# Reordered first loads, conditioning sums and weight splits in a fused mixer block

## The chip, the cores and the metric

The kernel runs on one core of a Trainium2 chip. The time is the device time of one execution in microseconds; three executions of the kernel before gave 1876.54, 1878.39 and 1878.52 us, with a median of 1878.39 us. Everything is float32 in and out.

## The reference: what is computed

One layer over a sequence of 4096 rows of 1024 numbers. A conditioning vector c makes a shift, a scale and a gate for each of the 1024 columns, each a product of silu(c) with a third of w_ada (1024 x 3072). The rows are normalised, scaled and shifted, and go through one wide projection; two branches (causal pooling, and a chunkwise recurrent memory with four heads) read its columns; their outputs are joined, projected by w_out, gated, added to x and normalised again.

```python
mod = jax.nn.silu(c) @ w_ada[l] + b_ada[l]
shift, scale, gate = jnp.split(mod, 3, axis=-1)
h = rms_norm(x, norm_g[l]) * (1.0 + scale[:, None, :]) + shift[:, None, :]
proj = h @ w_in[l]
...
x = x + gate[:, None, :] * (mix @ w_out[l])
```

## The kernel before, in words

The sequence is cut into 8 blocks of 512 rows. For each block the normalised, modulated rows are turned so that columns lie on partitions (`hT`), multiplied with `w_in` tile by tile, run through the branches and multiplied with `w_out`. Large products are made of three passes: a value is split into a rounded high part and a low part (the rest), and high x high, high x low and low x high are added. So each weight tile and each piece of `hT` has a high part, made by ScalarE (`split_w`, `hi_first`), and a low part, made by GpSimd (`low_w`, `lo_first`), in this order.

Each engine has its own instruction stream, written out by hand, and streams meet at semaphores. Nothing reorders them: an engine that waits holds everything behind it. The change touches only what is done once, before and during the first product of the first block. There the streams are these.

SyncE issues nearly all loads, and its queue moves them in the order of issue: the constants `cst`; seven small parameter vectors into rows of `hm` (`norm_g`, `c`, `b_ada`, `conv_w`, `conv_b`, `ls_pool`, `mh_norm_g`, L391); x's row chunks 0 and 1 (L371); groups 0 and 1 of w_ada (`load_ada`, L396, 1 MB each); x's chunks 2 and 3; group 2; the raw V weights 0 and 1 (`load_raw`, L336 for the small gate columns and L344); group 3; V weights 2 and 3; and then groups 4 to 7 and V weights 4 to 7 in turns. Chunks 2 and 3 wait until ScalarE has squared a first and a second chunk.

Groups 0 to 3 of w_ada make the shift and scale of columns 0 to 511, groups 4 to 7 those of columns 512 to 1023. A group has 8 row tiles of 128. VectorE folds tiles 0 to 4 into one by scaling with silu(c) (`sum_ada`: one multiplication, L1239, and four multiply-adds, L1242), and TensorE multiplies tiles 5, 6 and 7 with silu(c) (L540) and adds the folded tile through a product with ones (L543). It does so for two column halves of a group, one after the other, and waits for VectorE's sum before the first L543. The constant `ADA_SUMMED = 5` is the number of folded tiles.

VectorE's stream, in order: variance of chunks 0 and 1 (`prep_var`, L1187), sums of groups 0 and 1, variance of chunks 2 and 3, sums 2 and 3, `modulation(0)` (L1253 to L1257), `full_first(0)` and `(1)`, sum 4, `full_first(2)`, sum 5, `full_first(3)`, sums 6 and 7, `modulation(1)`, `full_first(4)` to `(7)`, then the sums of the gate. `full_first(i)` (L1270) applies scale and shift to one turned chunk half.

ScalarE: the tanh of silu(c) (L836), which needs the parameters; squares of chunks 0 and 1 (L826), their scaling (L841); squares of chunks 2 and 3, their scaling; splits of V weights 0 to 3; then the high parts of the chunk halves (L846), with one further V weight split (L822) before each of the halves 2 to 5. GpSimd follows with the low parts (L1083, L1108) in the same order.

TensorE: transposes of chunks 0 and 1, `ada(0)` (groups 0, 1), `ada(1)` (2, 3), three transposes, V weights 0 to 3 on chunks 0 and 1, `ada(2)` (4, 5), V weights 0 to 3 on chunks 2 and 3 with `ada(3)` (6, 7) after the second, and so on to the end of V; then the tiles of q.

Of the kernel before, what the change touches and what calls it, by code (L numbers as in the profile page):

```python
# [34 lines left out]
P = 128  # L35
D = 1024
KT = D // P
# [17 lines left out]
V_HELD = 4  # L55
UNITS = V_UNITS + 2 * 24
TILE_UNITS = V_UNITS + 32
ADA_SUMMED = 5
TASKS = 32
TANHS = 20  # L60
SCO_FULLS = 8
# [5 lines left out]
PREPS = 8  # L67
# [57 lines left out]
def build(nc, x, c, norm_g, w_ada, b_ada, w_in, b_gates, conv_w, conv_b, w_pool, ls_pool, mh_norm_g,  # L125
# [4 lines left out]
    with ExitStack() as ctx:  # L130
# [135 lines left out]

        gate_sum = x_in[:, 1, :]

        w_in_v = w_in[0].rearrange("(k p) n -> p k n", p=P)
        w_ada_v = w_ada[0].rearrange("(k p) n -> p k n", p=P)  # L270
        def reach(eng, sem, value):
# [45 lines left out]
        def _(sp):  # L317
# [45 lines left out]
            def load_x(nb, c, setup=False):  # L363

                dst = x_in
                if not setup:
                    sp.wait_ge(x_T, nb * PREPS + (2 * c - 2))
                elif c >= 2:
                    sp.wait_ge(x_sq_done, c - 1)
                    dst = x_res  # L370
                sp.dma_start(dst[:, c % 2, :], x[0, bass.ds(nb * BLK + c * P, P), :]).then_inc(x_loaded[c % 2], 16)  # L371
# [8 lines left out]
                sp.dma_start(out[0, bass.ds(b * BLK + j * P, P), :], normed[:, j % 2, :]).then_inc(stored[j % 2], 16)  # L380

            sp.dma_start(cst[:, :], consts[:, 0:K_END]).then_inc(cst_loaded, 16)
            rows = hm[:, 0, :]
            sp.wait_ge(rows_zeroed, 1)
            for at, src in ((C_NG, norm_g[0].rearrange("(t p) -> t p", p=P)), (C_C, c[0].rearrange("(t p) -> t p", p=P)),
                            (C_BA, b_ada[0].rearrange("(t p) -> t p", p=P)),
                            (C_CW, conv_w[0].rearrange("j (t p) -> (j t) p", p=P)),
                            (C_CB, conv_b[0].rearrange("(t p) -> t p", p=P)),
                            (C_LS, ls_pool[0].rearrange("(t p) -> t p", p=P)),
                            (C_MG, mh_norm_g[0].rearrange("(t p) -> t p", p=P))):  # L390
                sp.dma_start(rows[at:at + src.shape[0], :], src).then_inc(par_loaded, 16)  # L391

            def load_ada(g):
                half, pair = g % 2, g // 2
                off = D * half + 256 * pair
                sp.dma_start(ada_raw[:, g, :, :], w_ada_v[:, :, off:off + 256]).then_inc(ada_loaded[g], 16)  # L396
# [10 lines left out]
            load_x(0, 1, True)  # L407
            load_ada(0)
            load_ada(1)
            load_x(0, 2, True)  # L410
            load_x(0, 3, True)
            load_ada(2)
            load_raw(0)
            load_raw(1)
            load_ada(3)
            load_raw(2)
            load_raw(3)
            load_ada(4)
# [89 lines left out]
        def _(pe):  # L508
# [23 lines left out]
            def ada(s):  # L532

                for g in (2 * s, 2 * s + 1):
                    pe.wait_ge(ada_loaded[g], 16)
                    for t in range(2):
                        at = 8 * (s // 2) + 4 * (g % 2) + 2 * (s % 2) + t
                        dst = acc[1][:, at:at + 1]
                        for k in range(ADA_SUMMED, KT):
                            pe.matmul(dst, ada_raw[:, g, k, chunk(t)], silu_c[:, k:k + 1], start=k == ADA_SUMMED, stop=False)  # L540
                        if t == 0:
                            pe.wait_ge(ada_summed, g + 1)
                        last = pe.matmul(dst, ada_raw[:, g, 0, chunk(t)], ones[:, :], start=False, stop=True)  # L543
                    last.then_inc(ada_used, 1)
# [268 lines left out]
        def _(act):  # L813
# [18 lines left out]
                               ACT.Copy).then_inc(h_hi, 1)  # L832


            act.wait_ge(par_ready, 1)
            act.activation(tanh[:, 0:KT], par[:, C_C:C_C + KT], ACT.Tanh, scale=0.5).then_inc(c_tanh, 1)  # L836
            act.wait_ge(silu_c_ready, 1)
# [10 lines left out]
            for half in range(2):  # L848
# [2 lines left out]
                    prep_sq(0, c, (x_in, x_res)[half])  # L851
                for c in (2 * half, 2 * half + 1):
                    scale_first(c)
            for m in range(4):
                split_w(m)
            for i in range(PREPS):
                if i in (2, 3, 4, 5):
                    split_w(i + 2)
                hi_first(i)

            def wout_high(k):
                act.wait_ge(wout_scaled, k + 1)
# [213 lines left out]
        @block.gpsimd  # L1076
        def _(pool):
            def low_w(m, b=0):
                if m not in (RAW_NO if b == 0 else KEEP_SECOND):
                    return  # L1080
                pool.wait_ge(w_hi_done, split_no(b, m) + 1)
                hi, lo = halves(m)
                nc.gpsimd.tensor_tensor(w_split[:, slot(m), lo], w_raw[:, slot(m), lo],  # L1083
                                        w_split[:, slot(m), hi].bitcast(F32), ALU.subtract).then_inc(w_lo_done, 1)

            def prep_lo(nb, p):
                pool.wait_ge(h_hi, nb * PREPS + (p + 1))
                dst = slice(4 * (p % 2), 4 * (p % 2) + 4), chunk(p // 2)
                nc.gpsimd.tensor_tensor(hT_lo[:, dst[0], dst[1]], full[p % 2][:, :, :], hT_hi[:, dst[0], dst[1]].bitcast(F32),
                                        ALU.subtract).then_inc(h_lo, 1)  # L1090

            def rsqrt(var_done, value, dst, src, done):
                n = src.shape[1]
                pool.wait_ge(var_done, value)
                nc.gpsimd.tensor_tensor(dst, src, mhalf[:, 0:n], ALU.pow).then_inc(done, 1)  # L1095

            def x_rsqrt(nb, c):
                rsqrt(x_var_done, nb * NC + (c + 1), x_rs[:, c % 2:c % 2 + 1], x_var[:, c % 2:c % 2 + 1], x_rs_done)

            nc.gpsimd.memset(mhalf[:, :], -0.5).then_inc(mhalf_ready, 1)  # L1100
            pool.wait_ge(mhalf_ready, 1)
            for c in range(NC):
                x_rsqrt(0, c)
            def lo_first(i):
                c, half = i % NC, i // NC
                pool.wait_ge(h_hi, i + 1)
                dst = slice(4 * half, 4 * half + 4), chunk(c)
                nc.gpsimd.tensor_tensor(hT_lo[:, dst[0], dst[1]], full[i % 2][:, :, :], hT_hi[:, dst[0], dst[1]].bitcast(F32),  # L1108
                                        ALU.subtract).then_inc(h_lo, 1)

            for m in range(4):
                low_w(m)
            for i in range(PREPS):
                if i in (2, 3, 4, 5):
                    low_w(i + 2)
                lo_first(i)

            def one_block(b, last_block, first=False, second=False):
                def h_rsqrt(j):
                    rsqrt(h_var_done, b * NC + (j + 1), h_rs[:, :], h_var[:, :], h_rs_done)  # L1120

                if first:
                    for m in range(V_UNITS, 44):
                        low_w(m)
                if second:
                    for m in KEEP_SECOND:
                        low_w(m, 1)
                for j in range(NC):
                    m = 44 + 4 * j
                    if j > 0:  # L1130
                        h_rsqrt(j - 1)
                    for n in range(m, m + 4):
                        if first and n < UNITS:
                            low_w(n)
                        if n == m + 2 and j >= 2 and not last_block:
                            x_rsqrt(b + 1, j - 2)
                h_rsqrt(3)
                for i in range(8):
                    if i % 2 == 0 and not last_block:
                        prep_lo(b + 1, i)  # L1140
                        prep_lo(b + 1, i + 1)
                    if i in (1, 3) and not last_block:
                        x_rsqrt(b + 1, 2 + i // 2)
                    if i % 2:
                        j = i // 2
                        rsqrt(o_var_done, b * NC + (j + 1), o_rs[:, j % 2:j % 2 + 1], o_var[:, j % 2:j % 2 + 1], o_rs_done)

            one_block(0, False, True)
            for b in range(1, NB - 1):
                one_block(b, False, second=b == 1)  # L1150
            one_block(NB - 1, True)
# [3 lines left out]
        def _(dve):  # L1155
# [78 lines left out]
            def sum_ada(g):  # L1234

                buf = ada_raw[:, g, :, :]
                in_turn()
                dve.wait_ge(ada_loaded[g], 16)
                step(V.tensor_scalar(buf[:, 0, :], buf[:, 0, :], silu_c[:, 0:1], None, ALU.mult))  # L1239
                for k in range(1, ADA_SUMMED):  # L1240
                    in_turn()
                    ins = V.scalar_tensor_tensor(buf[:, 0, :], buf[:, k, :], silu_c[:, k:k + 1], buf[:, 0, :], ALU.mult, ALU.add)  # L1242
                    if k < ADA_SUMMED - 1:
                        step(ins)
                ins.then_inc(ada_summed, 1)
                did(ada_summed, g + 1)
# [503 lines left out]
```

## Time and profile before

| | |
|---|---|
| Median of three executions | 1878.39 us |
| The profiled execution | 1879.74 us |
| Its span in the trace | 1877.9 us |
| Around the span | 1.84 us |
| TensorE busy | 1831.1 us, 98% |
| VectorE busy | 1080.2 us, 58% |
| ScalarE busy | 477.6 us, 25% |
| GpSimd busy | 260.7 us, 14% |
| Granted TensorE clock, mean | 0.994 of full |

The slices of the profile show TensorE at 9 tenths or more in all but the first two of forty and the last; each slice is 47 us long. The opening is where the engines wait for each other and for loads, and it is the only place that the change touches.

### The profile page before, as it was taken

The numbers are of one execution on the slowest core, as the hardware profiler recorded it, in microseconds if no ns is written. First come the engines' busy times: TensorE is split into PE (matmuls) and PEld (weight loads), VectorE is DVE, ScalarE is ACT, GpSimd is POOL, SyncE is SP. The second block draws the span as 40 slices with busy tenths as digits, with TensorE's granted clock in tenths as the row PEclk, the third lists the DMA queues.
The fourth block names the chain that finished last, engine by engine and source line by source line (L and its number), as shares of the span: only waits on it lengthen the run. The fifth ranks groups of instructions, "written<-read, shape, count | busy, mean of one in ns | idle before, by whom it ended". The sixth has DMA issues, their size and how long they took to land.

```text
span 1877.9 us, 25194 instructions
## 1 busy us (share of the span) xinstructions
PE 1831.1 (98%) x9601; PEld 1567.9 (83%) x9601; DVE 1080.2 (58%) x2404; ACT 477.6 (25%) x990; POOL 260.7 (14%) x229
## 2 busy tenths in 40 slices
PE   6989999999999999999999999999999999999998
PEld 5877888878898888988888888888889888898886
DVE  6786674646737276363864547453673727636373
ACT  3225331232212122222232123222221212222221
POOL 3433222040220002100030001300022000210000
PEclk9899999999999999999999999999999999999999
DMA  9785634584256542664426642366425654266421
GB/s 330 267 302 162 200 121 155 178 295 170 76 195 191 179 148 79 214 191 159 145 85 233 194 173 91 136 219 206 146 75 196 191 179 149 78 215 191 136 98 68
DMA packets 134620, 319.94 MB, mean 170 GB/s; under 512 B 11788, under 2 KB 53476, under 8 KB 134500
## 3 DMA queue, kind: packets, MB, share of 16 engines
q1 hardware_dynamic: 129028, 312.56, 50.1%
q10 hardware_dynamic: 5472, 5.77, 0.9%
q8 instruction: 76, 1.25, 0.3%
q14 instruction: 44, 0.36, 0.1%
HBM read 272.09 MB, written 46.20 MB: 169 GB/s over the span
## 4 chain that ended last, share of the span: by engine, by line
PE 77%; DVE 16%; issue 3%; ACT 2%; DMA 1%; POOL 0%; SPq 0%; ACTq 0%; DVEq 0%; POOLq 0%
PE ps_acc L511 20%; PE ps_acc L513 20%; PE ps_acc L512 20%; DVE sb_acc_cv L1459 2%; PE ps_kv L511 1%; PE ps_kv L512 1%; PE ps_kv L513 1%; PE ps_sco L709 1%; DVE sb_shifted L1602 1%; PE ps_num L524 1%; PE ps_num L737 1%; PE ps_kv L741 1%; PE ps_num L736 1%; PE ps_num L511 1%; PE ps_num L513 1%
## 5 line engine op out<-in xcount | busy, mean ns | idle before, releaser
L511 PE MATMUL ps_acc<-sb_hT_hi,sb_w_split 128*128 128x512 f32 x1536 | 603.9, 393 | 2.2 <-DVE sb_oz L1479 1.6
L513 PE MATMUL ps_acc<-sb_hT_hi,sb_w_split 128*128 128x512 f32 x1536 | 599.3, 390 | 0.0
L512 PE MATMUL ps_acc<-sb_hT_lo,sb_w_split 128*128 128x512 f32 x1536 | 599.1, 390 | 0.0
L513 PEld LDWEIGHTS ps_acc<-sb_hT_hi,sb_w_split 128*128 128x128 f32 x1536 | 288.8, 188 | 61.6
L511 PEld LDWEIGHTS ps_acc<-sb_hT_hi,sb_w_split 128*128 128x128 f32 x1536 | 289.5, 188 | 60.8 <-DVE sb_oz L1479 2.0
L512 PEld LDWEIGHTS ps_acc<-sb_hT_lo,sb_w_split 128*128 128x128 f32 x1536 | 289.3, 188 | 59.3
L1095 POOL TENSOR_TENSOR sb_h_rs<-sb_h_var,sb_mhalf 128x4 f32<-128x4 f32 x32 | 32.4, 1012 | 1029.1 <-DVE sb_h_var L1553 1029.1
L1459 DVE SCALAR_TENSOR_TENSOR sb_acc_cv<-sb_shifted,sb_par,sb_acc_cv 128x512 f32<-128x512 f32 x192 | 148.0, 771 | 6.8
L1083 POOL TENSOR_TENSOR sb_w_split<-sb_w_raw,sb_w_split 128x512 fp32r<-128x512 f32 (+1 forms) x64 | 88.0, 1392 | 192.9 <-ACT sb_w_split L822 192.8
L1485 DVE TENSOR_TENSOR sb_oz<-sb_tanh,sb_oz 128x512 f32<-128x512 f32 x32 | 22.2, 693 | 150.4 <-ACT sb_tanh L969 150.4
L511 PE MATMUL ps_acc<-sb_wo_hi,sb_mixm_hi 128*128 128x512 f32 x256 | 103.1, 403 | 0.0
L511 PE MATMUL ps_acc<-sb_wo_hi,sb_mixp_hi 128*128 128x512 f32 x256 | 100.5, 392 | 1.7 <-DVE sb_mixp_lo L1572 1.7
L513 PE MATMUL ps_acc<-sb_wo_hi,sb_mixm_lo 128*128 128x512 f32 x256 | 100.0, 391 | 0.0
L513 PE MATMUL ps_acc<-sb_wo_hi,sb_mixp_lo 128*128 128x512 f32 x256 | 99.8, 390 | 0.0
L512 PE MATMUL ps_acc<-sb_wo_lo,sb_mixm_hi 128*128 128x512 f32 x256 | 99.8, 390 | 0.0
L512 PE MATMUL ps_acc<-sb_wo_lo,sb_mixp_hi 128*128 128x512 f32 x256 | 99.6, 389 | 0.0
L959 ACT ACTIVATE sb_tanh<-sb_acc_cv 128x512 f32<-128x512 f32 x64 | 40.5, 632 | 206.9 <-DVE sb_acc_cv L1459 206.9
L1674 DVE TENSOR_TENSOR sb_x_res<-ps_acc,sb_x_res 128x512 f32<-128x512 f32 x64 | 44.3, 692 | 62.3 <-PE ps_acc L513 42.6
L511 PE MATMUL ps_kv<-sb_w_split,sb_hT_hi 128*128 128x256 f32 x256 | 73.2, 286 | 3.1 <-POOL sb_hT_lo L1108 3.1
L993 ACT ACTIVATE sb_tanh<-sb_hm 128x128 bf16<-128x128 f32 x128 | 38.0, 298 | 140.1 <-DVE sb_hm L1535 140.1
L512 PE MATMUL ps_kv<-sb_w_split,sb_hT_hi 128*128 128x256 f32 x256 | 72.7, 284 | 0.0
L513 PE MATMUL ps_kv<-sb_w_split,sb_hT_lo 128*128 128x256 f32 x256 | 72.3, 282 | 0.0
(228 smaller groups left out, 2878.9 us busy)
## 6 DMA issues: line engine op xcount, KB each, us to landing
sb_w_split<-w_kept SPq DMA_DIRECT2D x328, 512.0 KB, 3.6
sb_w_split<-w_kept SPq DMA_DIRECT2D x56, 520.0 KB, 4.6
w_kept<-sb_w_split SPq DMA_DIRECT2D x40, 512.0 KB, 4.9
sb_x_res<-x SPq DMA_DIRECT2D x34, 512.0 KB, 5.3
sb_w_raw<-w_in SPq DMA_DIRECT2D x64, 256.0 KB, 4.4
out<-sb_qT SPq DMA_DIRECT2D x32, 512.0 KB, 2.9
sb_x_in<-x SPq DMA_DIRECT2D x30, 512.0 KB, 5.3
sb_ada_raw<-w_ada SPq DMA_DIRECT2D x8, 1024.0 KB, 9.7
```

Source lines behind the costliest of these rows:

```text
L511: pe.matmul(dst, st_hi, mv_hi, start=start, stop=False)
L512: pe.matmul(dst, st_hi, mv_lo, start=False, stop=False)
L513: return pe.matmul(dst, st_lo, mv_hi, start=False, stop=stop)
L524: last = pe.transpose(num[p % 2][:, chunk(i)], src[:, c % 2, chunk(k)], ident)
L709: last = pe.matmul(sco[:, chunk(h)], kT[:, h, chunk(j)], qT[:, h, chunk(j)], start=True, stop=True)
L959: act.activation(tanh[:, :], acc_cv[:, HALO:], ACT.Tanh, scale=0.5).then_inc(tanh_ready, 1)
L993: last = act.activation(junk[:, chunk(h)], hm[:, h, :], ACT.Square, accum_out=h_sq[:, h:h + 1])
L1083: nc.gpsimd.tensor_tensor(w_split[:, slot(m), lo], w_raw[:, slot(m), lo], w_split[:, slot(m), hi].bitcast(F32), ALU.subtract).then_inc(w_l ...
L1095: nc.gpsimd.tensor_tensor(dst, src, mhalf[:, 0:n], ALU.pow).then_inc(done, 1)
L1459: ins = V.scalar_tensor_tensor(acc_cv[:, HALO:], sh[:, HALO - 3 + n:HALO - 3 + n + BLK], tap[n], acc_cv[:, HALO:], ALU.mult, ALU.add)
L1485: V.tensor_tensor(oz[:, i, :], tanh[:, :], oz[:, i, :], ALU.mult).then_inc(free, 1)
L1674: V.tensor_tensor(x_res[:, j % 2, s], src[:, :], x_res[:, j % 2, s], ALU.add).then_inc(free, 1)
```

## The change

```diff
-ADA_SUMMED = 5
+ADA_SUMMED = [4, 4, 4, 4, 5, 5, 5, 5]
...
             sp.dma_start(cst[:, :], consts[:, 0:K_END]).then_inc(cst_loaded, 16)
-            rows = hm[:, 0, :]
-            sp.wait_ge(rows_zeroed, 1)
-            for at, src in (... the seven parameter vectors ...):
-                sp.dma_start(rows[at:at + src.shape[0], :], src).then_inc(par_loaded, 16)
...
             load_x(0, 1, True)
             load_ada(0)
             load_ada(1)
+            load_raw(0)
+            load_ada(2)
+            load_raw(1)
+            load_ada(3)
             load_x(0, 2, True)
             load_x(0, 3, True)
-            load_ada(2)
-            load_raw(0)
-            load_raw(1)
-            load_ada(3)
             load_raw(2)
...
# TensorE's ada(s) and VectorE's sum_ada(g): ADA_SUMMED becomes ADA_SUMMED[g]
...
# ScalarE, ahead of its first wait
+            rows = hm[:, 0, :]
+            act.wait_ge(rows_zeroed, 1)
+            for at, src in par_rows:
+                act.dma_start(rows[at:at + src.shape[0], :], src).then_inc(par_loaded, 16)
...
# ScalarE; GpSimd has the same with low_w and lo_first
-            for m in range(4):
-                split_w(m)
-            for i in range(PREPS):
-                if i in (2, 3, 4, 5):
-                    split_w(i + 2)
-                hi_first(i)
+            for i in range(0, PREPS, 2):
+                for m in {0: (0, 1), 2: (2, 3), 4: (4, 5, 6, 7), 6: ()}[i]:
+                    split_w(m)
+                hi_first(i)
+                hi_first(i + 1)
```

The seven parameter loads go from SyncE's queue to ScalarE's. On SyncE's, V weight 0, group 2, V weight 1 and group 3 now stand ahead of x's chunks 2 and 3. VectorE folds four tiles instead of five in groups 0 to 3, and TensorE multiplies four instead of three. The V weights are split two before the chunk halves 0 and 1, two before 2 and 3, and four before 4 and 5. VectorE's order of work is as it was.

## Rows read from the trace of the kernel before

**Rows 1.** The page: engines' busy time, and the chain of waits by engine.

```profile
PE 1831.1 (98%) x9601; PEld 1567.9 (83%) x9601; DVE 1080.2 (58%) x2404; ACT 477.6 (25%) x990; POOL 260.7 (14%) x229
PE 77%; DVE 16%; issue 3%; ACT 2%; DMA 1%; POOL 0%; SPq 0%; ACTq 0%; DVEq 0%; POOLq 0%
```

**Rows 2.** Waits of TensorE, 0 to 74 us: total, times, longest, in us.

```profile
PE ps_num L556 <- ACT sb_x_in L841: 5.8, 1, 5.8
PE ps_acc L543 <- DVE sb_ada_raw L1242: 4.0, 2, 3.1
```

**Rows 3.** Timeline of SyncE's queue: start, duration, what it issues.

```profile
1.19 0.36 SPq L391 DMA_DIRECT2D sb_hm<-norm_g  x1
...
3.68 0.83 SPq L371 DMA_DIRECT2D sb_x_in<-x  x2
```

**Rows 4.** Chain of waits in order of time: start, duration, what.

```profile
4.08 4.61 DMA sb_x_in<-x
...
15.11 9.68 DMA sb_ada_raw<-w_ada
...
29.90 1.28 PE ps_acc L540 x6
...
47.08 0.64 ACT sb_hT_hi L846
```

**Rows 5.** Timeline of VectorE; in brackets the wait before and what ended it.

```profile
11.79 0.36 DVE L1239 TENSOR_SCALAR sb_ada_raw<-sb_ada_raw,sb_silu_c 128x256 f32<-128x256 f32 x1 [1.62 <-DMA sb_ada_raw<-w_ada]
12.19 2.05 DVE L1242 SCALAR_TENSOR_TENSOR sb_ada_raw<-sb_ada_raw,sb_silu_c 128x256 f32<-128x256 f32 x4
...
18.59 0.15 DVE L1187 TENSOR_SCALAR sb_x_var<-sb_x_sq 128x1 f32<-128x1 f32 x1 [1.13 <-ACT sb_tanh L826]
...
31.72 0.16 DVE L1253 TENSOR_TENSOR sb_shift<-ps_acc,sb_par 128x4 f32<-128x4 f32 x1 [2.46 <-PE ps_acc L543]
...
41.77 3.88 DVE L1242 SCALAR_TENSOR_TENSOR sb_ada_raw<-sb_ada_raw,sb_silu_c 128x256 f32<-128x256 f32 x4
...
58.46 0.16 DVE L1253 TENSOR_TENSOR sb_shift<-ps_acc,sb_par 128x4 f32<-128x4 f32 x1 [4.67 <-PE ps_acc L543]
```

**Rows 6.** Timeline of TensorE.

```profile
4.81 0.45 PE L530 MATMUL ps_acc<-sb_cst,sb_hm 128*128 128x128 f32 x1 [4.81 <-DMA sb_hm<-mh_norm_g]
...
12.96 1.27 PE L540 MATMUL ps_acc<-sb_silu_c,sb_ada_raw 128*128 128x1 f32 x6
...
29.32 0.59 PE L543 MATMUL ps_acc<-sb_ones,sb_ada_raw 128*128 128x1 f32 x2 [0.93 <-DVE sb_ada_raw L1242]
...
45.44 0.81 PE L540 MATMUL ps_acc<-sb_silu_c,sb_ada_raw 128*128 128x1 f32 x6
46.11 0.36 PE L543 MATMUL ps_acc<-sb_ones,sb_ada_raw 128*128 128x1 f32 x2
...
56.08 0.56 PE L543 MATMUL ps_acc<-sb_ones,sb_ada_raw 128*128 128x1 f32 x2
```

**Rows 7.** Timeline of ScalarE.

```profile
7.47 1.06 ACT L826 ACTIVATE sb_tanh<-sb_x_in 128x1024 bf16<-128x1024 f32 x1 [1.12 <-DMA sb_x_in<-x]
...
17.34 1.06 ACT L826 ACTIVATE sb_tanh<-sb_x_res 128x1024 bf16<-128x1024 f32 x1
```

**Rows 8.** Timeline of GpSimd.

```profile
42.08 1.32 POOL L1108 TENSOR_TENSOR sb_hT_lo<-sb_dmat,sb_hT_hi 128x512 fp32r<-128x512 f32 x1 [3.48 <-ACT sb_hT_hi L846]
43.37 1.47 POOL L1083 TENSOR_TENSOR sb_w_split<-sb_w_raw,sb_w_split 128x520 fp32r<-128x520 f32 x1
```

**Rows 9.** Stretches: busy time of each engine, granted clock, DMA share, GB/s.

```profile
2.50:5.00 2.50, 0.19 (x1) 0.18 (x1) 1.83 (x8) 0.00 (x0) 0.00 (x0) 1.00 0.33 59
...
20.00:25.00 5.00, 1.63 (x7) 1.55 (x8) 4.37 (x6) 1.84 (x3) 2.70 (x2) 1.00 1.09 350
```

**Rows 10.** Issues by line, 164 to 170 us, then 150 to 156 us: us to landing.

```profile
w_kept<-sb_mixm_lo ACTq DMA_DIRECT2D x1, 256.0 KB, 5.7
...
w_kept<-sb_mixm_lo ACTq DMA_DIRECT2D x1, 256.0 KB, 2.8
```

More of the change, by code:

```diff
@@ L267, in build @@
         gate_sum = x_in[:, 1, :]
+        par_rows = ((C_NG, norm_g[0].rearrange("(t p) -> t p", p=P)), (C_C, c[0].rearrange("(t p) -> t p", p=P)),
+                    (C_BA, b_ada[0].rearrange("(t p) -> t p", p=P)),
+                    (C_CW, conv_w[0].rearrange("j (t p) -> (j t) p", p=P)),
+                    (C_CB, conv_b[0].rearrange("(t p) -> t p", p=P)),
+                    (C_LS, ls_pool[0].rearrange("(t p) -> t p", p=P)),
+                    (C_MG, mh_norm_g[0].rearrange("(t p) -> t p", p=P)))
         w_in_v = w_in[0].rearrange("(k p) n -> p k n", p=P)
@@ L382, in _ @@
             sp.dma_start(cst[:, :], consts[:, 0:K_END]).then_inc(cst_loaded, 16)
-            rows = hm[:, 0, :]
-            sp.wait_ge(rows_zeroed, 1)
[L385 to L390, printed above, removed]
-                sp.dma_start(rows[at:at + src.shape[0], :], src).then_inc(par_loaded, 16)
             def load_ada(g):
@@ L538, in ada @@
                         dst = acc[1][:, at:at + 1]
-                        for k in range(ADA_SUMMED, KT):
-                            pe.matmul(dst, ada_raw[:, g, k, chunk(t)], silu_c[:, k:k + 1], start=k == ADA_SUMMED, stop=False)
+                        for k in range(ADA_SUMMED[g], KT):
+                            pe.matmul(dst, ada_raw[:, g, k, chunk(t)], silu_c[:, k:k + 1], start=k == ADA_SUMMED[g], stop=False)
                         if t == 0:
@@ L1109, in lo_first @@
                                         ALU.subtract).then_inc(h_lo, 1)
[L1111 to L1115, printed above, removed]
+            for i in range(0, PREPS, 2):
+                for m in {0: (0, 1), 2: (2, 3), 4: (4, 5, 6, 7), 6: ()}[i]:
+                    low_w(m)
                 lo_first(i)
+                lo_first(i + 1)
             def one_block(b, last_block, first=False, second=False):
@@ L1239, in sum_ada @@
                 step(V.tensor_scalar(buf[:, 0, :], buf[:, 0, :], silu_c[:, 0:1], None, ALU.mult))
-                for k in range(1, ADA_SUMMED):
+                for k in range(1, ADA_SUMMED[g]):
                     in_turn()
                     ins = V.scalar_tensor_tensor(buf[:, 0, :], buf[:, k, :], silu_c[:, k:k + 1], buf[:, 0, :], ALU.mult, ALU.add)
-                    if k < ADA_SUMMED - 1:
+                    if k < ADA_SUMMED[g] - 1:
                         step(ins)
```

## The prediction

> **What bounds the kernel now.** The page comes first: TensorE is busy 98% of the span and carries 77% of the chain that ended last [rows 1]. So after the opening there is nothing to win by this change; it can only move the moment at which the steady work begins. I then read TensorE's waits in the first 74 us [rows 2]: 5.8 us for the first scaled chunk of x and 4.0 us for VectorE's folded tiles. The chain of waits in order of time [rows 4] says what lies under them: the load of x, then the load of w_ada's group 3, which lands at 15.11 + 9.68 = 24.79, the sum on VectorE, TensorE's small products, and from there VectorE's stream up to ScalarE's high part at 47.08. Past 24.79 no transfer stands in that chain for hundreds of microseconds; sums, convolutions on VectorE and TensorE follow each other. I therefore take a shift of that chain to arrive at the end one for one.
>
> **When x's chunks land.** Between the landing of x's chunk 1 at 4.08 + 4.61 = 8.69 and that of group 3 at 24.79 lie 16.1 us. In them SyncE's queue carried groups 0 to 3 (4 x 1024 KB), chunks 2 and 3 (2 x 512) and V weights 0 and 1 (2 x 260): 5640 KB, 350 KB a microsecond, the same as the 350 GB/s of the stretch 20 to 25 [rows 4, 9]. This queue is full, and order alone says what lands when. The change takes seven issues from before x: x is issued at 1.19 instead of 3.68, 2.49 us earlier [rows 3]. The constants (192 KB, 0.5 us at that rate) are then directly ahead of x, which may take back up to 0.5. In the new order chunk 3 has in front of it, itself included, exactly the 5640 KB that group 3 closed before. So chunk 3 lands at 24.79 - 2.49 = 22.3 to 22.8; I take 22.6. Before, ScalarE squared it from 17.34 [rows 7]: it comes 5.3 us later. Group 3 lands 2 x 512 KB earlier than that, near 19.7, chunk 2 near 21.1.
>
> **The sums, step 1.** VectorE's order has the variances of chunks 2 and 3 ahead of sums 2 and 3, and the change leaves that. Before, the square began at 17.34, the variance at 18.59 and ended at 18.74 [rows 5, 7]; with 0.1 to the next instruction, sum 2 can start 1.5 us after chunk 3. That is 24.1, though group 2 has been there for eight microseconds. One sum cost 0.36 + 2.05 with its gap, 2.45 from 11.79 to 14.24 [rows 5]; with one multiply-add of 0.51 less it is 1.94, so sum 2 is done at 26.1.
>
> **TensorE behind it, step 2.** One small product takes 1.28 / 3 = 0.427 us [rows 4]. A group now has 2 x 5 products, 4.27 us, instead of 3.42. From 12.96 [rows 6] groups 0 and 1 take until 21.5, the four products of group 2's first half until 23.2, and there TensorE waits until 26.1, 2.9 us. Left then are the folded tile, five products of the second half and ten of group 3: 16. Before, from the L543 at 29.32 there were five left and the modulation began at 31.72, 2.40 later [rows 5, 6]. Eleven more cost 4.69, so the modulation begins at 26.1 + 2.40 + 4.69 = 33.2. Sum 3 (until about 29 with two splits on GpSimd beside it) is not late for its product at 30.2. **Step 1 and 2 together: +1.5 us.** The price of the fourth product, 8 x 0.427 = 3.4 us, is what the earlier loads had to pay for, and chunk 3 doesn't let them.
>
> **The splits, step 3.** Four multiply-adds take 2.05 us alone, from 12.19, and 3.88 when two GpSimd operations run beside them, the low part at 42.08 and the split at 43.37 [rows 5, 8]: 0.9 for each. Now V weights 2 and 3 fall into sum 4 (one GpSimd operation more, +0.9), and sum 5 loses one (-0.9), so `full_first(3)` is on time. On the way TensorE reads sum 5 for group 5's first half, at 46.11 + 1.5 = 47.6 [rows 6], with the sum ready at 41.77 + 3.88 + 1.5 = 47.2 [rows 5]: 0.4 to spare. V weights 2 and 3 are split by 41.5, before TensorE comes to them. Then weights 4 to 7 are split in one go: sum 6 starts at 47.08 + 1.5 = 48.6 [rows 4], and GpSimd runs from 49.3 to 49.3 + 1.3 + 4 x 1.47 = 56.5. Five of its operations stand beside sums 6 and 7, against two before (the same pair as beside sum 5). Sum 7 is done at 48.6 + 2 x 2.47 + 5 x 0.9 = 58.0. TensorE wants it at 56.08 + 1.5 = 57.6 [rows 6]. **Step 3: +0.5 us** with the hand-over. From `modulation(1)` (58.46 before, 60.4 after) nothing changes but the missing split between halves 4 and 5, and nobody was held by it: by the order of the streams `full_first(5)` waits for a transpose that TensorE does behind V's products.
>
> The Trainium skill (SBUF — State Buffer, Who interferes with whom) has VectorE and GpSimd take a shared port by turns, each fully blocking the other for an instruction. The trace shows a loss of 0.9 us for a GpSimd operation of 1.32 to 1.47 [rows 5, 8], so less than the whole. What full blocking would make of the sum is a rival below.
>
> **The parameters, step 4.** ScalarE has nothing to do before they are there, so its seven issues cost nothing themselves. Before, the squares at 7.47 waited 1.12 us for x [rows 7]. Part of that idle time went to VectorE's silu(c), which the squares wait for too; so I give the parameters half a microsecond, and TensorE's products another 2.9 (its new wait at 23.2). They had landed by 4.81 [rows 6]. They may be 3.4 us later, at 8.2, before anything moves. Price between 0 and the rival's: I take 0, as the first of them are issued before x's bytes move (the stretch from 2.5 to 5 carries 59 GB/s [rows 9]).
>
> **The sum.** +1.5 + 0.5 = +2.0 us. The profiled execution would have a span of 1879.9 and take 1881.7 (1879.74 + 2.0); it lies 1.35 over the median of the runs, and against the median of 1878.39 I say 1880.4.
>
> **Rivals.** A: chunk 3 doesn't hold the sums. Then TensorE runs its 40 products from 12.96 without a stop, modulation at 12.96 + 17.1 + 0.27 = 30.3, -1.4, and with step 3 -0.9: 1877.5. It needs chunk 3 by 19.7, three microseconds under the queue's rate. For it speaks that TensorE idled 4.0 us on sums [rows 2], against it the order on VectorE. Chance 0.14, with all that lies between.
>
> B, the slow one: the parameters' small transfers wait behind x and w_ada on the same sixteen engines. It decides from 8.2 on. If the last lands with group 0, near 9.4, TensorE begins 4.0 later than before and 1.1 of it shows: 1881.5. If it lands with group 1, 12.4, it is +4.1 more: 1885.6. A transfer of ScalarE's queue took 5.7 us beside a busy SyncE queue and 2.8 in a quieter stretch [rows 10]; but these were 256 KB, not 2 to 16. Chance 0.15, a third of it for the long case.
> By the Trainium skill (DMA: Bandwidth & Descriptors, Queues, rings and completion order) a transfer engine alternates between queues a whole packet at a time, so that a small transfer does wait behind x's packets; no row here separates packets.
>
> C: GpSimd blocks VectorE for its whole operation. Three more of them cost 3 x 1.3 to 1.47 instead of 3 x 0.9, sum 7 is done 1.2 to 1.7 later, all of it TensorE's wait: 1881.8. Chance 0.10. That is the skill's rule of the shared port at its word.
>
> D: TensorE's clock rises in the longer run of products. Later a product takes half as long, (46.11 - 45.44) / 3 = 0.22 [rows 6]: 16 of them save 3.3, the sum is -1.3: 1877.1. Before, products ran from 12.96 to 21.7 without a stop at 0.427, so 0.04. It and A together could give 1875.
>
> **Chances.** Forecast 0.57, A 0.14, B 0.15, C 0.10, D 0.04. A measurement of this kernel tells about 0.2% from no change, 3.8 us: 1874.6 to 1882.2. Forecast, A and C lie inside, so does B's short case. Faster 0.03; slower 0.12 (B's long case, parts of B and C together); same 0.85. The range of 8 in 10 is 1876.4 to 1883.6: A and D with a microsecond of the runs' own spread below them, and B's middle above.
>
> **What would show it.** VectorE's first multiplication of group 2 at 24 with a wait for ScalarE's square, not for a load; chunk 3 squared from 22.3 to 22.8; modulation at 33.2 and 60.4; eight records of L540 before each L543 instead of six; sums 6 and 7 ending near 58, TensorE waiting some tenths for it. Wrong: modulation before 31.7 (A or D), squares of chunk 0 after 10.9 (B), or a first q tile that does not move with the modulation, which would break the one-for-one.

## The result, and the profile after

| | before | after |
|---|---|---|
| Median of 11 executions | 1878.79 us (1876.54 to 1880.01) | 1882.12 us (1880.91 to 1883.50) |
| Ratio, 95% interval | | 1.0016 (1.0009 to 1.0024) |
| Span of the profiled execution | 1877.9 us | 1879.2 us |

The change makes the kernel slower by 0.16%, 3.0 us, with 1.7 to 4.5 us as the interval. 1880.4 was forecast, 2.0 us over the median then known, with a range up to 1883.6. The spans of the two profiled executions lie only 1.3 us apart; why is told behind the timelines.

What happened in the opening can be followed in five views of the changed kernel. First VectorE's timeline (start, duration, line, operation; in brackets the wait before it and what ended it), to be laid beside [rows 5].

```profile
13.13 0.15 DVE L1186 TENSOR_SCALAR sb_x_var<-sb_x_sq 128x1 f32<-128x1 f32 x1 [1.03 <-ACT sb_tanh L822]
13.32 0.38 DVE L1238 TENSOR_SCALAR sb_ada_raw<-sb_ada_raw,sb_silu_c 128x256 f32<-128x256 f32 x1
...
15.69 1.52 DVE L1241 SCALAR_TENSOR_TENSOR sb_ada_raw<-sb_ada_raw,sb_silu_c 128x256 f32<-128x256 f32 x3
23.01 0.15 DVE L1186 TENSOR_SCALAR sb_x_var<-sb_x_sq 128x1 f32<-128x1 f32 x1 [5.80 <-ACT sb_tanh L822]
24.34 0.15 DVE L1186 TENSOR_SCALAR sb_x_var<-sb_x_sq 128x1 f32<-128x1 f32 x1 [1.17 <-ACT sb_tanh L822]
24.52 0.38 DVE L1238 TENSOR_SCALAR sb_ada_raw<-sb_ada_raw,sb_silu_c 128x256 f32<-128x256 f32 x1
24.94 1.53 DVE L1241 SCALAR_TENSOR_TENSOR sb_ada_raw<-sb_ada_raw,sb_silu_c 128x256 f32<-128x256 f32 x3
...
33.61 0.16 DVE L1252 TENSOR_TENSOR sb_shift<-ps_acc,sb_par 128x4 f32<-128x4 f32 x1 [3.19 <-PE ps_acc L539]
...
49.14 4.77 DVE L1241 SCALAR_TENSOR_TENSOR sb_ada_raw<-sb_ada_raw,sb_silu_c 128x256 f32<-128x256 f32 x4
53.95 1.29 DVE L1238 TENSOR_SCALAR sb_ada_raw<-sb_ada_raw,sb_silu_c 128x256 f32<-128x256 f32 x1
55.27 2.95 DVE L1241 SCALAR_TENSOR_TENSOR sb_ada_raw<-sb_ada_raw,sb_silu_c 128x256 f32<-128x256 f32 x4
60.67 0.16 DVE L1252 TENSOR_TENSOR sb_shift<-ps_acc,sb_par 128x4 f32<-128x4 f32 x1 [2.45 <-PE ps_acc L539]
```

Sum 1 ends at 17.2 and VectorE then idles 5.80 us, not for w_ada but for ScalarE's square of chunk 2 and then 1.17 for chunk 3; sum 2 starts at 24.52 without a wait of its own. The two modulations (the rows that write `sb_shift`) begin at 33.61 and 60.67; before it was 31.72 and 58.46 [rows 5]. In sums 6 and 7 five of the ten operations are stretched: sum 6's four multiply-adds take 4.77 us where they take 2.05 alone, sum 7's multiplication takes 1.29 where it takes 0.35 to 0.38 alone, and its four multiply-adds take 2.95.

TensorE's timeline of the same stretch, beside [rows 6].

```profile
8.64 0.45 PE L526 MATMUL ps_acc<-sb_cst,sb_hm 128*128 128x128 f32 x1 [8.64 <-DMA sb_hm<-mh_norm_g]
14.21 2.06 PE L552 MATMUL ps_num<-sb_cst,sb_x_in 128*128 128x128 f32 x8 [5.12 <-ACT sb_x_in L842]
16.07 1.71 PE L536 MATMUL ps_acc<-sb_silu_c,sb_ada_raw 128*128 128x1 f32 x8
...
26.52 0.58 PE L539 MATMUL ps_acc<-sb_ones,sb_ada_raw 128*128 128x1 f32 x2 [0.21 <-DVE sb_ada_raw L1241]
...
58.27 0.58 PE L539 MATMUL ps_acc<-sb_ones,sb_ada_raw 128*128 128x1 f32 x2 [0.35 <-DVE sb_ada_raw L1241]
```

The parameters arrive only by 8.64 (4.81 before [rows 6]), so the products start at 16.07 instead of 12.96. They then run almost without a stop: of the 4.0 us that TensorE waited for sums [rows 2] 0.6 is left. And yet the first modulation is later, since the start is later and there is one product more in each of the eight half groups.

The chain of waits in order of time shows the two loads that set this, and GpSimd's timeline what stretches sums 6 and 7.

```profile
3.46 5.05 DMA sb_hm<-mh_norm_g
...
14.66 8.34 DMA sb_x_res<-x
```

```profile
49.45 1.30 POOL L1108 TENSOR_TENSOR sb_hT_lo<-sb_k_w,sb_hT_hi 128x512 fp32r<-128x512 f32 x1 [3.47 <-ACT sb_hT_hi L847]
50.71 5.67 POOL L1083 TENSOR_TENSOR sb_w_split<-sb_w_raw,sb_w_split 128x520 fp32r<-128x520 f32 x4
```

Chunk 3 lands at 23.00. From 49.45 to 56.38 GpSimd has no gap. The gates are read after V at 81.63 against 79.44 before. I use three marks from here: the first modulation (31.72 before, 33.61 changed), the second (58.46, 60.67) and the first read of the gates (79.44, 81.63). Each comes from one execution, and they do not repeat exactly: among the kernels below that load the parameters alike, TensorE could start on them between 8.31 and 9.31.

The shift is still 2.3 us at 243 us and half of that at 297. The same two variances on VectorE show it, before and then changed:

```profile
243.24 0.15 DVE L1187 TENSOR_SCALAR sb_x_var<-sb_x_sq 128x1 f32<-128x1 f32 x1
296.60 0.15 DVE L1187 TENSOR_SCALAR sb_x_var<-sb_x_sq 128x1 f32<-128x1 f32 x1 [7.37 <-ACT sb_tanh L826]
```

```profile
245.54 0.15 DVE L1186 TENSOR_SCALAR sb_x_var<-sb_x_sq 128x1 f32<-128x1 f32 x1
297.64 0.15 DVE L1186 TENSOR_SCALAR sb_x_var<-sb_x_sq 128x1 f32<-128x1 f32 x1 [7.23 <-ACT sb_tanh L822]
```

The changed kernel is 2.30 us behind at the first and 1.04 at the second. Between them lies a stretch in which TensorE's clock differs; its columns are the stretch, its length, the busy time of TensorE, its weight loads, VectorE, ScalarE and GpSimd, the granted clock, the DMA share and GB/s. Before, and then the same work in the changed kernel:

```profile
246.90:250.30 3.40, 3.40 (x14) 2.92 (x13) 3.19 (x13) 1.28 (x8) 0.00 (x0) 0.51 0.38 106
```

```profile
248.90:252.30 3.40, 3.40 (x19) 2.98 (x20) 3.23 (x12) 1.12 (x8) 0.00 (x0) 1.00 0.36 118
```

So the profiled execution of before lost about 1.1 us to a stretch at half clock that the profiled execution of the changed kernel did not have. A time can move by a microsecond in this way, whatever the opening does. Why the clock fell in the one and not in the other is open.

### The profile page after: what moved, and what is told of

Its sections match the earlier page's. It is cut to its first block, busy times and chain, and to the rows that moved or that the text cites. A ratio compares the mean times of both kernels' runs of the same rounds, so it can differ in the third digit from the quotient of the medians.

```text
span 1879.2 us, 25222 instructions
## 1 busy us (share of the span) xinstructions
PE 1832.2 (98%) x9617; PEld 1569.4 (84%) x9617; DVE 1079.0 (57%) x2400; ACT 477.3 (25%) x990; POOL 260.6 (14%) x229
## 4 chain that ended last, share of the span: by engine, by line
PE 76%; DVE 17%; issue 3%; ACT 2%; DMA 1%; POOL 0%; ACTq 0%; SPq 0%; DVEq 0%; POOLq 0%
PE ps_acc L507 20%; PE ps_acc L509 20%; PE ps_acc L508 20%; DVE sb_acc_cv L1458 2%; PE ps_kv L507 1%; PE ps_kv L508 1%; PE ps_kv L509 1%; PE ps_sco L705 1%; DVE sb_shifted L1601 1%; PE ps_num L520 1%; DVE sb_ada_raw L1241 1%; DVE sb_acc_cv L1601 1%; DVE sb_mixp_lo L1571 1%; PE ps_num L733 1%; PE ps_kv L737 1%
## 5 line engine op out<-in xcount | busy, mean ns | idle before, releaser
L507 PEld LDWEIGHTS ps_acc<-sb_hT_hi,sb_w_split 128*128 128x128 f32 x1536 | 289.1, 188 | 60.6 <-DVE sb_oz L1478 2.0
```

The lines of the kernel that those rows point to most:

```text
L507: pe.matmul(dst, st_hi, mv_hi, start=start, stop=False)
```

## The experiments

All timed runs stand beside runs of the kernel before on the same chip, whose medians were 1878.55 to 1879.01 us. Times are device microseconds; marks come from one profiled execution each. I call a wall what holds the first modulation when everything else is early enough; the working theory of the experiments is that two walls stand close together, VectorE's sums behind chunk 3 and TensorE's small products behind the parameters.

| kernel | first modulation | second | gates | median | ratio to before, 95% |
|---|---|---|---|---|---|
| before | 31.72 | 58.46 | 79.44 | | |
| changed | 33.61 | 60.67 | 81.63 | 1882.12 | 1.0016 (1.0009, 1.0024) |
| e1 parameters alone | 33.21 | 59.94 | 80.92 | 1881.12 | 1.0011 (1.0002, 1.0021) |
| e2 parameters back | 35.60 | 62.06 | 82.94 | 1883.23 | 1.0024 (1.0013, 1.0034) |
| e3 variances late | 33.75 | 60.14 | 80.91 | 1881.21 | 1.0013 (1.0004, 1.0023) |
| e4 splits back | 35.58 | 61.93 | 82.93 | 1882.02 | 1.0017 (1.0008, 1.0027) |
| e5 x held | 36.42 | 63.48 | 84.47 | 1883.62, one run | |
| e6 squares first | 29.88 | 56.95 | 77.92 | 1877.36 | 0.9995 (0.9986, 1.0004) |
| e7 and five tiles | 26.55 | 54.01 | 74.98 | 1875.09 | 0.9981 (0.9972, 0.9990) |
| e8 and transposes first | 26.56 | 53.77 | 74.74 | 1874.26 | 0.9979 (0.9970, 0.9987) |
| e10 five tiles in the changed | 33.86 | 61.12 | 82.14 | 1881.64 | 1.0015 (1.0006, 1.0025) |

### e1: one part alone, the parameters on ScalarE's queue

The kernel before with this edit:

```diff
 SyncE, ahead of x:
-            sp.wait_ge(rows_zeroed, 1)
-                sp.dma_start(rows[at:at + src.shape[0], :], src).then_inc(par_loaded, 16)
 ScalarE, ahead of the tanh of c:
+            act.wait_ge(rows_zeroed, 1)
+            for at, src in par_rows:
+                act.dma_start(rows[at:at + src.shape[0], :], src).then_inc(par_loaded, 16)
```

> The kernel before with one part of the change: the seven parameter loads go to ScalarE's queue. Main theory (two walls: TensorE's small products behind the parameters, and sums behind the landing of loads): the parameters land 3.7 us late as in the changed kernel, near 8.5, TensorE's products start at 16.1 instead of 13.0 and run without a stop, 8 x 1.71 = 13.7, so the first modulation begins at 30.0 (before 31.72, changed 33.6), since all loads of w_ada come 2.3 earlier and no sum is late; the second modulation at 56.8, the time 1.7 us under the kernel before. Rival (the late parameters are what costs): everything starts 3.1 later, modulation at 34.8, time +3.

Measured: first modulation 33.21, ratio 1.0011. That is neither theory's number. TensorE's products started at 16.4 (16.1 expected), but it waited for sums again, because w_ada's groups came late. SyncE's queue and the stretches of this kernel (busy time of each engine, clock, DMA share, GB/s) show why.

```profile
2.13 1.06 SPq L392 DMA_DIRECT2D sb_ada_raw<-w_ada  x2
12.23 1.52 SPq L377 DMA_DIRECT2D sb_x_res<-x  x2
13.80 0.43 SPq L392 DMA_DIRECT2D sb_ada_raw<-w_ada  x1
...
17.68 0.56 SPq L392 DMA_DIRECT2D sb_ada_raw<-w_ada  x1
```

```profile
7.50:10.00 2.50, 0.44 (x1) 0.18 (x1) 0.44 (x4) 0.00 (x0) 0.00 (x0) 1.00 1.09 366
...
12.50:15.00 2.50, 0.42 (x2) 0.46 (x3) 1.40 (x4) 2.50 (x4) 1.11 (x2) 1.00 0.60 198
15.00:17.50 2.50, 2.50 (x14) 2.23 (x12) 2.32 (x6) 1.62 (x3) 0.00 (x0) 1.00 0.89 252
```

SyncE issues nothing between 3.2 and 12.23. In the order of before, chunk 2 is issued once ScalarE has squared chunk 0; the squares wait for silu(c), this for the parameters, and these are late. What had been issued runs out: 198 GB/s in the stretch from 12.5 to 15, where the kernel before had 379. Group 3 landed at 17.68 + 8.58 = 26.26, where 22.5 was expected (24.79 less 2.3). So this part alone costs twice, on TensorE and on the queue, and the new order of loads in the change hides the second payment, since it puts x's chunks behind group 3.

### e2 and e5: the parameters back on SyncE's queue, and x held until they are there

```diff
 e2, the seven loads on SyncE, ahead of x:
-                act.dma_start(rows[at:at + src.shape[0], :], src).then_inc(par_loaded, 16)
+                sp.dma_start(rows[at:at + src.shape[0], :], src).then_inc(par_loaded, 16)
 e5:
+            sp.wait_ge(par_loaded, 16 * 7)
             load_x(0, 0, True)
```

> The changed kernel with the parameter loads back on SyncE's queue ahead of x. Main theory: parameters land by 4.8 again, but chunk 3 lands 2.5 later, at 25.5, sum 2 starts at 27.0, and the first modulation begins at 36.1 (changed 33.6): time 2.5 us over the changed kernel, about 5 to 6 over before. Rival (late parameters cost the changed kernel its 2 to 3 us): modulation at 32 or earlier, time as before or less.

> The changed kernel, but SyncE holds x and all behind it until the seven parameter loads have landed. It asks why these land 3.7 us late. Theory (rival B's mechanism: small transfers share the engines with x): with nothing beside them they land near 4.9, as before, x is issued at 5.1, chunk 3 lands near 27, modulation at 37.5. Rival (ScalarE's queue is itself slow at the start of the program, or its issues are): they land at 8.5 again, and x after that.

Both kernels' TensorE waits for the parameters, e2's row and then e5's:

```profile
5.07 0.45 PE L531 MATMUL ps_acc<-sb_cst,sb_hm 128*128 128x128 f32 x1 [5.07 <-DMA sb_hm<-mh_norm_g]
```

```profile
4.94 0.45 PE L527 MATMUL ps_acc<-sb_cst,sb_hm 128*128 128x128 f32 x1 [4.94 <-DMA sb_hm<-mh_norm_g]
```

e5 decides why the parameters are late in the change. They are on ScalarE's queue in both; with x held back they are there at 4.94, with x beside them at 8.64. The 3.7 us are the price of x and w_ada moving beside them, not of ScalarE's queue; that the price comes from sharing the transfer engines is likely, but no row separates it. In e2 the first modulation moved to 35.60 (36.1 expected) and in e5 to 36.42 (37.5): parameters on time and a slower kernel. That refutes the rival: with the parameters on time the changed kernel is set by the arrival of chunk 3, and parameters in front of x delay it. Both runs delay the whole queue; no run puts the old order of x's chunks back alone. In e2 chunk 3 was squared from 25.07 on, 2.0 later than in the changed kernel (23.08) and not 2.5: the half microsecond of the constants, which are ahead of x in the changed order, is the likely difference.

### e3: the sums no longer wait for x

```diff
+            sum_ada(2)
+            sum_ada(3)
             prep_var(0, 2)
             prep_var(0, 3)
-            sum_ada(2)
-            sum_ada(3)
```

> The changed kernel with VectorE's variances of chunks 2 and 3 put behind sums 2 and 3, so that the sums wait for their own loads alone. Main theory: the second wall stands right behind the first. TensorE's 40 products from 16.07 need 17.1 + 0.3, so the modulation begins at 33.4 instead of 33.6 and the time moves by 0.2 us, nothing that can be measured; sums 2 and 3 are done by 22. Rival (VectorE's order alone holds the sums, step 1 of the prediction taken alone): modulation at 31 or earlier, time 2 to 3 us less than the changed kernel.

VectorE's row at the first modulation:

```profile
33.75 0.16 DVE L1252 TENSOR_TENSOR sb_shift<-ps_acc,sb_par 128x4 f32<-128x4 f32 x1 [9.12 <-PE ps_acc L539]
```

First modulation 33.75, no earlier than the changed kernel's 33.61, and a ratio of 1.0013 beside 1.0016, which are not told apart. The theory's number was 33.4 (this execution's parameters were 0.5 later, at 9.15). VectorE's wait of 5.80 us for the squares is gone and the first modulation gains nothing, because TensorE's 40 products from 16.6 on end no sooner; VectorE now waits 9.12 us for them. VectorE's longest wait was worth nothing at this mark: two walls stood within a few tenths of each other.

The second modulation (60.14 for 60.67) and the gates (80.91 for 81.63) did come earlier. TensorE's clock accounts for it at least in part: the last small products ran at the high level here (granted clock 1.00 from 57.1 to 59.5) and at the low one in the changed kernel (0.50 from 59.0 to 60.4). The rows are those of group 7's second half, e3's and then the changed kernel's.

```profile
58.90 0.81 PE L536 MATMUL ps_acc<-sb_silu_c,sb_ada_raw 128*128 128x1 f32 x6
```

```profile
58.72 1.42 PE L536 MATMUL ps_acc<-sb_silu_c,sb_ada_raw 128*128 128x1 f32 x6
```

So differences of half a microsecond in the last two marks are not read as effects of an edit below, unless the rows show the wait.

### e6, e7, e8: both walls moved

e6 is e3 with ScalarE's order changed, and the same for VectorE's variances:

```diff
 ScalarE:
-            act.wait_ge(par_ready, 1)
-            act.activation(tanh[:, 0:KT], par[:, C_C:C_C + KT], ACT.Tanh, scale=0.5).then_inc(c_tanh, 1)
-            act.wait_ge(silu_c_ready, 1)
...
             for half in range(2):
+                if half:
+                    act.wait_ge(silu_c_ready, 1)
...
                     scale_first(c)
+                if not half:
+                    act.wait_ge(x_sq_done, 2)
+                    act.wait_ge(par_ready, 1)
+                    act.activation(tanh[:, 0:KT], par[:, C_C:C_C + KT], ACT.Tanh, scale=0.5).then_inc(c_tanh, 1)
 VectorE:
+            prep_var(0, 0)
+            prep_var(0, 1)
             dve.wait_ge(par_T, 1)
```

e7 adds `ADA_SUMMED = [5] * 8`; e8 moves TensorE's waits for silu(c) and the parameters behind the transposes of chunks 0 and 1.

> Kernel e3 (variances 2 and 3 behind the sums) with ScalarE's squares and scaling of chunks 0 and 1, and VectorE's variances of them, ahead of the parameters, so that x no longer waits for silu(c). Two walls theory: with the second wall moved as well, TensorE's 40 products start at 11.1 instead of 16.1; first modulation at 28.6, second at 55.7, gates read at 76.6 (before 79.44), time 2.8 us under the kernel before, 5 under the changed one. Rival (loads of w_ada or x become the wall at once): modulation at 32 or later, time as the changed kernel.

> Kernel e6 with five folded tiles in all groups as before the change. Theory: TensorE's products are the wall in e6, so 8 x 0.427 = 3.4 us of them less shows almost whole: first modulation at 25.3, second at 53, gates read at 74, time 5.5 us under the kernel before. Rival (VectorE's sums are the wall, as the four tiles suppose): modulation where e6 has it or later. A second rival, chunk 3 and its splits on ScalarE become the wall, would show as high parts of hT waiting for nothing but ScalarE's own splits, and half of the gain gone by the second modulation.

TensorE in e6 and in e7:

```profile
10.94 1.97 PE L552 MATMUL ps_num<-sb_cst,sb_x_in 128*128 128x128 f32 x8 [1.81 <-DVE sb_silu_c L1233]
12.71 1.71 PE L536 MATMUL ps_acc<-sb_silu_c,sb_ada_raw 128*128 128x1 f32 x8
...
29.21 0.57 PE L539 MATMUL ps_acc<-sb_ones,sb_ada_raw 128*128 128x1 f32 x2
```

```profile
12.79 1.28 PE L536 MATMUL ps_acc<-sb_silu_c,sb_ada_raw 128*128 128x1 f32 x6
...
25.88 0.56 PE L539 MATMUL ps_acc<-sb_ones,sb_ada_raw 128*128 128x1 f32 x2
```

In e6 the products run from 12.71 to 29.64 without one wait: 40 at 0.42. The first modulation came 3.9 earlier than in e3 and 3.7 earlier than in the changed kernel, where 5 were expected: I had overlooked that TensorE's transposes stand behind the same wait for silu(c) and start at 10.94 instead of 9.1. The time is not told from the kernel before (0.9995, with 1 in the interval), where 2.8 us less was expected. In e7 the products take from 12.79 to 26.3. Eight fewer gave 3.33 us at the first modulation (3.4 expected) and 2.94 at the gates. With both walls gone TensorE's products are the third, and the fourth tile that the change gave it costs its full price. e7 is faster than both kernels: 0.9981 (0.9972 to 0.9990), 3.6 us under before, 6.7 under the changed kernel by the gates. Its marks are about a microsecond later than expected (26.55, 54.01 and 74.98 for 25.3, 53 and 74), as they were worked out from e6's expected marks, and 5.5 us under before was expected for its time.

> Kernel e7 with TensorE's wait for silu(c) moved behind the transposes of chunks 0 and 1. In e7 these began only at 11.0, with silu(c), though x was scaled by 10.4. Theory: the products start at 11.3 instead of 12.8, the first modulation 1.5 earlier (25.0), but behind it GpSimd is busy without a break with splits and low parts up to 35, and sum 4 beside it ends at 35.5 instead of 35.9, so that of the 1.5 only 0.4 is left at the second modulation (53.6) and at the gates (74.6). Rival (what starts earlier ends earlier): 52.5 and 73.5, time 1.5 us under e7.

```profile
11.47 1.41 PE L536 MATMUL ps_acc<-sb_silu_c,sb_ada_raw 128*128 128x1 f32 x6
13.92 0.58 PE L539 MATMUL ps_acc<-sb_ones,sb_ada_raw 128*128 128x1 f32 x2 [1.03 <-DVE sb_ada_raw L1245]
```

e8's products start 1.3 earlier and then wait 1.03 us for sum 0, which silu(c) delays: the first modulation is where it was. Part of that wait is this execution's: its parameters came at 9.31, in e7's at 8.31, and its sum 0 began 0.4 later than e7's. With e7's parameters some tenths would be left of the 1.5 us that was expected, by this estimate. My reason (GpSimd behind the modulation) did not come to the test, as nothing came earlier for it to swallow. The gates moved 0.24, and the times (1874.26 and 1875.09) are not told apart.

### e4 and e10: the splits and the fourth product, each undone in the changed kernel

```diff
 e4, ScalarE, and GpSimd likewise:
+            for m in range(4):
+                split_w(m)
+            for i in range(PREPS):
+                if i in (2, 3, 4, 5):
+                    split_w(i + 2)
+                hi_first(i)
 e10:
-ADA_SUMMED = [4, 4, 4, 4, 5, 5, 5, 5]
+ADA_SUMMED = [5] * 8
```

> The changed kernel with the splits of V's weights in their old order on ScalarE and GpSimd. Main theory (a GpSimd operation costs a multiply-add beside it 0.9 us): the wait of 0.35 us for sum 7 goes, but two more splits fall beside sum 3, which ends 0.9 later, at 31.3, and TensorE wants it at 30.8: the first modulation 0.5 later (34.1), the second at 60.7 to 60.8, time within 0.3 us of the changed kernel. Rival (the pairs of splits cost the half microsecond of step 3 for nothing in return): second modulation at 60.2, 0.5 us less.

> The changed kernel with five folded tiles in all groups: the change of the sums undone alone. Theory: with sums 2 and 3 held until chunk 3 is squared, the tile that goes back to VectorE costs there what it saves on TensorE: sum 2 ends at 27.0, sum 3 with two splits beside it at 31.4, first modulation at 33.8 (changed 33.6), time within 0.3 us of the changed kernel. Rival (the fourth product is what made the change slower): modulation at 31 to 32, time 2 us less.

TensorE's wait for sum 3 in e4, the three multiply-adds of that sum, and VectorE's sum 3 in e10:

```profile
32.75 0.59 PE L539 MATMUL ps_acc<-sb_ones,sb_ada_raw 128*128 128x1 f32 x2 [0.44 <-DVE sb_ada_raw L1243]
```

```profile
28.26 4.44 DVE L1243 SCALAR_TENSOR_TENSOR sb_ada_raw<-sb_ada_raw,sb_silu_c 128x256 f32<-128x256 f32 x3
```

```profile
27.08 1.34 DVE L1238 TENSOR_SCALAR sb_ada_raw<-sb_ada_raw,sb_silu_c 128x256 f32<-128x256 f32 x1
28.45 2.95 DVE L1241 SCALAR_TENSOR_TENSOR sb_ada_raw<-sb_ada_raw,sb_silu_c 128x256 f32<-128x256 f32 x4
...
33.86 0.16 DVE L1252 TENSOR_TENSOR sb_shift<-ps_acc,sb_par 128x4 f32<-128x4 f32 x1 [2.45 <-PE ps_acc L539]
```

In e10 sum 3 ends at 31.4 and the modulation begins at 33.86 (31.4 and 33.8 expected), and the time is not told from the changed kernel's (1.0015 beside 1.0016). The same eight products that are worth 3.3 us in e7 are worth nothing where the sums wait for chunk 3. In e4 the marks lie 2.0 and 1.3 over the changed kernel's, but not by the splits: chunk 2 was squared from 23.10 in this execution, against 21.76 to 22.22 in the six others with this order of loads. Less that 1.3 they would be 34.3 and 60.6 (34.1 and 60.7 to 60.8 expected), though the second owes some tenths to products that ran at the high clock, as in e3. The multiply-adds of sum 3 took 4.44 us; in the changed kernel, with one split less beside them, 3.53: 0.91 for a GpSimd operation, as forecast. The other way round, the multiply-adds of sum 4 took 3.97 in e4 and 4.89 in the changed kernel. The wait for sum 7 is gone and one of 0.44 for sum 3 has come. So the trade is shown in the trace; the times, 1.0017 beside 1.0016, fit an even trade but can't tell half a microsecond.

## Why the prediction was right, point by point

- **The landing of chunk 3, and step 1.** 22.6 was said and 23.00 measured. Sum 2 at 24.52 (24.1 said) without a wait for its own load, ended at 26.47 (26.1). e2 and e5 push chunk 3 back and the modulation goes with it. Confirmed.
- **Step 2.** 7.1 us from there to the modulation were said; 26.52 to 33.61 is 7.09. The first modulation stands at 33.61 for 33.2, and the 0.4 is the chunk's. Sum 3 was put too early: about 29 was said, where the prediction's own terms give 26.1 + 1.94 + 2 x 0.9 = 29.8, and 30.42 was measured, with TensorE's product for it at 30.80 where 30.2 was said, so 0.4 us was left of the 1.2 in the prediction.
- **Step 3.** V weights 2 and 3 beside sum 4 were free: from the first modulation to V's second part on TensorE 17.2 us passed (50.81), and 17.2 in e4 with the old order; sums 6 and 7 ended at 58.2 for 58.0, TensorE waited 0.35 where 0.5 was said. A GpSimd operation beside VectorE costs 0.9 us of its 1.3 to 1.47, also in a row of five. Rival C is refuted: it wanted sum 7 at 59.2 or later, in an execution whose opening was on time. That was the rule of full blocking in the Trainium skill (SBUF — State Buffer, Who interferes with whom); the measured loss per operation is less than the operation.
- **Step 4, the parameters, was wrong in size.** I took 0 and they came 3.8 us later, rival B's mechanism, shown by e5. That they cost little was luck of the margin: products at 16.07 instead of 12.96 used 3.1 of the margin, and the wait that the prediction had there (2.9 us at 23.2) shrank to 0.21. The prediction let the parameters be late until 8.2; they came at 8.64 and still cost nothing. I had written the margin down but not that the change spends it whole. This is why e3 and e10, each of which takes away one of my steps, moved the first modulation by only 0.1 and 0.3 us. The rule of the Trainium skill that the prediction quoted for rival B (DMA: Bandwidth & Descriptors, Queues, rings and completion order) agrees with e5 in its direction, 8.64 with x beside and 4.94 without.
- **Rival A** is out in its words, as sum 2 waited for chunk 3; e3 shows that without that wait the late parameters would have kept its gain away. **D** is out too: a product took 0.427 us from 16.07 to 33.4. The prediction's reason for its low chance was a little off, as the products before did stop once, for 0.32 us at 20.31, where a group of w_ada was late.
- **The sum.** +2.0 was said, the marks give +2.2 and the times +3.0 (1.7 to 4.5). Over all kernels timed more than once the time lies up to 1.0 above the shift of the gates (-0.3 for e4, 0.1 for e10, 0.6 to 1.0 for the other seven). Every shift is counted from the one profiled execution of before, and there is no second trace of it: the difference is open.
- **One for one.** The prediction took the shift of the opening to arrive at the end whole. In the profiled pair it did so up to 245 us, and 1.3 us of it was left in the spans, as the half-clock stretch at 247 us came in one and not in the other. In the stretch from 235 to 260 us the mean granted clock was 0.93 in before, e1, e4, e6, e8 and e10 and 1.00 in the changed kernel, e2, e3, e5 and e7; in the latter five the shift of the span is 0.3 to 1.1 us less than that of the gates, in the other five it is within 0.3 us of it. Times near 1880 us therefore carry about a microsecond that no step of the prediction is about, and how often an execution of each kernel has this stretch is not known. That the sum came out near the measured time says less for the steps than their marks do.

## What to carry to other kernels

When an opening has three streams that must meet (here parameters, the small products behind them, and x behind the big loads), work out the arrival time of each in the new order before making any of them cheaper. A gain on one is worth nothing while another stands within a few tenths of it: the same eight products were worth 0 and 3.3 us at the first modulation, the same reorder of variances 0 alone and part of 4 together with an earlier start of the products. A load moved behind others also moves every wait that stands behind its consumer in the engines' order: moving x meant moving its variance too. And small transfers that a chain starts with come late when large loads move beside them. Landing them first made this kernel slower (e2, e5), as the large loads then came late; what paid was to let nothing wait for them but what truly needs them (e6, e7).

## What was not expected of the hardware

- Seven transfers of 2 to 16 KB on ScalarE's queue landed 1.5 us after the last issue when only the constants had been issued beside them (3.45 to 4.94 in e5), and 5.05 us after it with SyncE's queue full (3.46 to 8.51 in the changed kernel; TensorE could start on them at 8.31 to 9.31 in the eight kernels that had it so).
- A queue of loads that stood still for 9 us at its issuing engine (e1, 3.2 to 12.23) kept the transfer engines at 349 to 366 GB/s from 5 to 10, 284 to 12.5, and was down to 198 only from 12.5 on. Landings come 8 to 10 us after issues here (8.34, 8.58 and 9.68 in the rows), so a hold on the issuing side costs late and not where it stands.
- The column of the granted clock reads 1.00 from the start although the pace of the first products is that of the low level. Of the changed kernel, the stretch of the first products, two of V's products and one of the last small products:

```profile
16.00:33.00 17.00, 16.79 (x81) 16.71 (x79) 7.09 (x13) 5.43 (x8) 3.81 (x4) 1.00 1.08 359
38.90:40.10 1.20, 1.20 (x6) 1.19 (x6) 1.16 (x2) 0.00 (x0) 1.20 (x1) 1.00 1.03 408
41.00:45.00 4.00, 4.00 (x36) 4.00 (x35) 3.82 (x9) 0.63 (x1) 1.05 (x2) 1.00 1.02 406
...
59.00:60.40 1.40, 1.40 (x8) 1.40 (x8) 0.00 (x0) 0.00 (x0) 0.00 (x0) 0.50 1.03 344
```

The first and the last run at 0.427 us a product; the last says 0.50, the low level of 1.2 GHz, and the first 1.00. V's products take 0.20 us each up to 40.1 and 0.11 from 41 on, and both stretches say 1.00; the small products at 45.44 in the kernel before took 0.22 [rows 6]. So the column misleads up to about 40 us and agrees with the paces from there on. Up to there the pace of a known instruction is the better witness. A run of such products without a gap for 17 us (e6, 12.71 to 29.64) did not change their pace.
